# Head squares on ScalarE, a shared second query half, absorbed queries behind the prompt attention, and the gate third applied last

## What is computed

```
shift, scale, gate = split(silu(c) @ w_ada + b_ada)
h = rms(x) * (1 + scale) + shift
zq, zkv, zd, ga, gb, ma, mb = split(h @ w_in)
q      = rms(zq) @ w_qb            # 8 heads of 64 + 32, each part normalised, the 32 rotated
rows   = [rms(zkv[:256]), rope(rms(zkv[256:]))]        # latent and rotary key
dq, dk = rope(rms(zd)), dv = zd    # 3 dilated groups, 4 heads of 64
k_nope = rms(rows @ w_uk); v = rows @ w_uv
o_a    = attention(q, [k_nope, k_pe])   # prompt: causal; sample: 4096 cached rows per sequence
o_b    = dilated window attention over the 3 groups, combined
y      = x + gate * ((sigmoid(ma) * ((o_a*silu(ga)) @ w_pa) + sigmoid(mb) * ((o_b*silu(gb)) @ w_pb)) @ w_out)
```

## Time and profile before

| what | value |
|---|---|
| median of 3 runs | 1371.1 us (1368.76 to 1372.58) |
| time of the profiled execution | 1372.51 us |
| its span | 1370.7 us |
| mean granted TensorE clock | 0.913 |
| busy: PE, DVE, ACT, POOL | 89%, 52%, 36%, 19% of the span |
| chain that ended last, by engine | PE 57%, DVE 19%, issue 8%, ACT 5%, DMA 5%, POOL 4% |

### The profile page before, as it was taken

One profiled execution on the slowest core, in us unless ns is written; L12 is line 12 of the kernel. 1 busy time (PEld: TensorE's weight loads), 2 busy tenths in 40 slices (PEclk: granted clock), 3 DMA queues, 4 the chain that ended last, 5 costly groups with the idle time before them and its releaser, 6 DMA issues.

```text
span 1370.7 us, 22960 instructions
## 1 busy us (share of the span) xinstructions
PE 1219.1 (89%) x7616; PEld 998.1 (73%) x7616; DVE 715.8 (52%) x1657; ACT 495.2 (36%) x1159; POOL 254.7 (19%) x252
## 2 busy tenths in 40 slices
PE   5987758998897899999987999998999899997986
PEld 1277647786786678778765998988999899997431
DVE  4137887456865233030322676766676667676422
ACT  1133334332243333322322554545454545453010
POOL 0023330048865012333431000000000000000000
PEclk9989857999999657999998999999999999998579
DMA  8622010031242102233264310323232323225005
GB/s 262 220 77 72 23 41 1 13 81 47 73 127 77 31 23 71 77 101 85 71 199 159 96 31 22 88 62 88 61 86 64 88 61 83 66 75 184 1 20 166
DMA packets 79398, 112.24 MB, mean 82 GB/s; under 512 B 8627, under 2 KB 50756, under 8 KB 79293
## 3 DMA queue, kind: packets, MB, share of 16 engines
q1 hardware_dynamic: 76214, 101.59, 25.8%
q0 software_dynamic: 1440, 5.11, 1.0%
q10 hardware_dynamic: 1648, 4.23, 0.8%
HBM read 105.21 MB, written 5.68 MB: 81 GB/s over the span
## 4 chain that ended last, share of the span: by engine, by line
PE 57%; DVE 19%; issue 8%; ACT 5%; DMA 5%; POOL 4%; SPq 2%; ACTq 0%; DVEq 0%; POOLq 0%
PE ps L1376 18%; PE ps L1050 5%; PE ps L1051 5%; PE ps L1052 5%; PE ps L1357 5%; DVE ssq L2106 3%; PE ps L1065 3%; PE ps L1402 3%; DMA raw<-in_w_ada 2%; ACT cT_hi L850 2%; PE ps L1422 2%; PE ps L1212 1%; PE ps L1255 1%; POOL tmp L946 1%; PE ps L1266 1%
## 5 line engine op out<-in xcount | busy, mean ns | idle before, releaser
L931 POOL TENSOR_TENSOR wlo<-raw,whi 128x512 fp32r<-128x512 f32 (+3 forms) x148 | 172.1, 1165 | 459.8 <-ACT whi L620 459.6
L1376 PE MATMUL ps<-wq_hi,cT_hi 128*128 128x260 f32 x1024 | 217.8, 294 | 0.5 <-ACT sq L879 0.5
L1050 PE MATMUL ps<-whi,hT_hi 128*128 128x512 f32 (+3 forms) x512 | 190.3, 372 | 30.4 <-POOL wlo L931 19.2
L2106 DVE TENSOR_REDUCE ssq<-sq 128x8 f32<-128x512 f32 x256 | 172.6, 682 | 66.6 <-ACT sq L879 64.5
L1376 PE MATMUL ps<-wq_hi,cT_lo 128*128 128x260 f32 x1024 | 206.3, 283 | 0.0
L1376 PE MATMUL ps<-wq_lo,cT_hi 128*128 128x260 f32 x1024 | 206.0, 282 | 0.0
L620 ACT ACTIVATE whi<-raw 128x512 fp32r<-128x512 f32 (+3 forms) x148 | 83.3, 564 | 316.5 <-PE ps L1047 246.3
L1052 PE MATMUL ps<-whi,hT_lo 128*128 128x512 f32 (+3 forms) x512 | 185.8, 363 | 0.0
L1051 PE MATMUL ps<-wlo,hT_hi 128*128 128x512 f32 (+3 forms) x512 | 185.7, 363 | 0.0
L1376 PEld LDWEIGHTS ps<-wq_hi,cT_hi 128*128 128x128 f32 x1024 | 157.6, 190 | 1.1 <-ACT sq L879 1.1
L1376 PEld LDWEIGHTS ps<-wq_hi,cT_lo 128*128 128x128 f32 x1024 | 158.2, 189 | 0.0
(11 more groups left out here) (390 smaller groups left out, 1690.0 us busy)
## 6 DMA issues: line engine op xcount, KB each, us to landing
cn<-in_cache_mla SPq DMA_DIRECT2D x256, 144.0 KB, 2.1
raw<-in_w_in SPq DMA_DIRECT2D x64, 256.0 KB, 2.7
raw<-in_w_ada SPq DMA_DIRECT2D x48, 256.0 KB, 3.0
raw<-in_w_out SPq DMA_DIRECT2D x32, 256.0 KB, 3.0
sdk<-in_cw SPq DMA_DIRECT2D x3, 1536.0 KB, 11.0
raw<-in_w_in SPq DMA_DIRECT2D x32, 128.0 KB, 2.0
raw<-in_w_pa SPq DMA_DIRECT2D x16, 256.0 KB, 2.9
x_tiles<-in_x_prompt ACTq DMA_DIRECT2D x4, 512.0 KB, 5.6
```

Source lines behind the costliest of these rows:

```text
L931: nc.gpsimd.tensor_tensor(out=wlo[:, s % NHL, 0:width], in0=raw[:, j % NRAW, 0:width], in1=whi[:, s % NHL, 0:width].bitcast(F32), op=ALU.s ...
L1050: mm(out, hi[:, k, c], bh, start=st, stop=False)
L1376: last = mm(ps[:, 3 + 2 * (u % 2) + f, 0:260], a[c], wq[:, c, f, w], start=c == 0 and a is hi and wq is wq_hi, stop=c == 1 and a is lo)
L2106: v.tensor_reduce(out=ssq[:, (4 * g + u) * 8:(4 * g + u + 1) * 8], in_=sq4[:, u, :].rearrange("p (h e) -> p h e", e=NOPE), axis=AX, op=ALU ...
```

## The change

Four things are done:

- **Gate third last.** Shift and scale are turned once `ada0` to `ada3` are in; `ada4` and `ada5` follow on PE, and h is computed meanwhile. The gate matmuls and their two copies move behind the dilated projections. `gate_bc` now shares its memory with `wukT`, and `k_s` shares that of `dq_s`.
- **Squares on ScalarE.** For the prompt tiles of QB0, K, QB1 and the DgQK, ACT squares its own staged copy into one of two buffers, and DVE only sums. The sample tile stays on DVE. ACT also makes the rotary copies of the keys, and DVE rotates the key rows of the four prompt tiles at once.
- **Second query half shared.** POOL finishes tiles 1 and 3 of QB1 with `finish_q`, DVE tiles 0, 2 and TS, after it has scaled all five in the order 1, 0, 3, 2, TS.
- **Absorbed queries later.** The transposes stand behind the prompt attention, the 16 matmuls ahead of the fourth chunk of `D0QK`, and DVE's part behind the attention.

```diff
-          + [("gate", 2, "A"), ("Q", 5, "A"), ("KV", 5, "A"), ...
+          + [("Q", 5, "A"), ("KV", 5, "A"), ...
-STAGES += [("TD", 4 * (ND - 1), "A"), ...
+STAGES += [("gate", 2, "A"), ("TD", 4 * (ND - 1), "A"), ...
...
+            def to_stage_squared(idx, w):
+                k = staged[0]
+                to_stage(idx, w)
+                squared_[0] += 1
+                n = squared_[0]
+                act.wait_ge(evac_a, READER[idx][1])
+                if n > 2:
+                    act.wait_ge(square_free, n - 2)
+                nc.scalar.activation(squares[n % 2][:, 0:w], stage[:, k % NSTAGE, 0:w], ACT.Square).then_inc(squared, 1)
...
-            for n in range(2, 6):
+            for n in range(2, 4):
                 to_stage(ITEM[f"ada{n}"], 512, n=NB + 1)
-            split_to(FIRST["Q"] + NHL)
-            for n in range(2):
-                copy_out(ITEM["gate"] + n, gate_bc[:, n * 512:(n + 1) * 512], 512)
             for k in range(KD):
                 act.wait_ge(h_f, k + 1)
                 nc.scalar.activation(hThi[:, k, :], xT[:, k, :], ACT.Copy).then_inc(h_hi, 1)
+            for n in range(4, 6):
+                to_stage(ITEM[f"ada{n}"], 512, n=NB + 1)
...
+            act.wait_ge(rows_ready, 4)
+            for t in range(NT):
+                nc.scalar.activation(kc[:, t, :].rearrange("p (h e) -> p h e", e=QK)[:, :, NOPE:QK],
+                                     rep(rows[:, t, KVR:CW], 1, HM), ACT.Copy).then_inc(kc_rope, 1)
             for t in range(NT):
-                to_stage(ITEM["K"] + t, 512)
+                to_stage_squared(ITEM["K"] + t, 512)
...
                 for t in range(NT):
-                    to_stage(ITEM[f"D{g}QK"] + t, 512)
+                    to_stage_squared(ITEM[f"D{g}QK"] + t, 512)
...
+            finish_q(1, 1, Q_FREED + 10 + 1, qh1_pool, 1)
+            finish_q(1, 3, Q_FREED + 10 + 3, qh1_pool, 2)
...
+            def absorbed_queries(k):
+                if k != 3:
+                    return
+                misc_begin()
+                for odd in range(2):
+                    ...                       # the same 16 matmuls as before
             for g in range(ND):
-                block_of(f"D{g}QK", ITEM[f"D{g}QK"], range(5), hThi, hTlo, hTs)
+                block_of(f"D{g}QK", ITEM[f"D{g}QK"], range(5), hThi, hTlo, hTs,
+                         ahead_of=absorbed_queries if g == 0 else None)
...
+            for n in range(2):
+                idx = ITEM["gate"] + n
+                wait_bank(idx)
+                mm(ps[:, idx % BANKS, :], ident[0:NB + 1, NB:NB + 1].to_broadcast([NB + 1, P]),
+                   gate_s[:, n * 512:(n + 1) * 512], start=True, stop=True).then_inc(z_done, 1)
             heads_turned(0, ITEM["TD"])
...
-                link(v.tensor_tensor(out=sqt[0:n, :], in0=z, in1=z, op=ALU.mult))
-                link(v.tensor_reduce(out=ms[0:n, 8 * t:8 * t + 8], in_=sqt[0:n, :].rearrange("p (h e) -> p h e", e=64),
-                                     axis=AX, op=ALU.add))
+                sq3 = head_sums(t, z, 512).rearrange("p (h e) -> p h e", e=64)
+                sums_read(t, v.tensor_reduce(out=ms[0:n, 8 * t:8 * t + 8], in_=sq3, axis=AX, op=ALU.add))
...
-                for t in range(5):
+                for t in ((1, 0, 3, 2, TS) if i else range(5)):
                     q_item(i, t, zs[t])
+                if i:
+                    for n, t in enumerate((0, 2, TS)):
+                        q_finish(t, n + 1)
```

More of the change, by code:

```diff
@@ L753, in _ @@
             for t in range(NT):
[L754 removed]
+                squared_[0] += 1
+                n = squared_[0]
+                if n > 2:
+                    act.wait_ge(square_free, n - 2)
+                act.wait_ge(evac_a, READER[ITEM["QB0"] + t][1])
+                nc.scalar.activation(squares[n % 2][:, 0:384], stage[:, (k0 + t) % NSTAGE, 0:384], ACT.Square)\
+                  .then_inc(squared, 1)
+            act.wait_ge(rows_ready, 4)
+            for t in range(NT):
+                nc.scalar.activation(kc[:, t, :].rearrange("p (h e) -> p h e", e=QK)[:, :, NOPE:QK],
+                                     rep(rows[:, t, KVR:CW], 1, HM), ACT.Copy).then_inc(kc_rope, 1)
+            for t in range(NT):
+                to_stage_squared(ITEM["K"] + t, 512)
             to_stage_small(ITEM["K"] + TS, 512)
@@ L1671, in _ @@
             low_h(KD - 1)
+            for n in range(4, 6):
+                ada_item(n)
             v.tensor_tensor(out=g96[:, 0:NOPE], in0=gn[:, G_QN:G_QN + 64], in1=gn[:, G_KN:G_KN + 64], op=ALU.mult)
@@ L1847, in _, with set_q @@
             attention(MLA_JOBS, 0, 0, 4, 2, mla_mask, mla_place, MLA_SCALE)
+            misc_wait()
+            v.tensor_copy(qsT[:, :], ps[:, 7, 0:32])
+            link(v.memset(qpe[:, :], 0.0))
+            for u in range(4):
+                last = v.tensor_copy(qpe[32 * u:32 * u + 32, :].rearrange("p (b u h) -> p u h b", b=NB, u=4)[:, u],
+                                     ps[0:ROPE, 7, 32:96].rearrange("p (h b) -> p h b", b=NB))
+            misc_read(last)
+            misc_wait()
+            misc_read(v.tensor_copy(qabs[:, 0:NB * 16].rearrange("p (b c h) -> p c h b", c=2, b=NB),
+                                    ps[:, 7, 0:128].rearrange("p (c h b) -> p c h b", c=2, b=NB)))
+            link(v.memset(qabs[:, NB * 16:(NB + 1) * 16], 0.0))
+            def set_q(b, p, step):
+                q3 = qabs[:, bass.ds(16 * b, 16)].rearrange("p (c f h) -> p c f h", c=2, f=2)
+                cols_ = slice(260 * p, 260 * p + 4)
+                step(v.tensor_copy(wq_hi[:, :, :, cols_], q3))
+                return v.tensor_tensor(out=wq_lo[:, :, :, cols_], in0=q3, in1=wq_hi[:, :, :, cols_].bitcast(F32),
+                                       op=ALU.subtract)
+            for b in range(2):
+                link(set_q(b, b, link))
+            dve.wait_ge(kc_ready, 5)
+            own = tmp_t[0:NB, 1792:2560]
+            link(v.tensor_tensor(out=own, in0=q_s[:, :], in1=k_s[:, :], op=ALU.mult))
+            link(v.tensor_reduce(out=dns[:, :], in_=own.rearrange("p (h e) -> p h e", e=QK), axis=AX, op=ALU.add))
+            link(v.tensor_tensor(out=snew[:, :].rearrange("p (b h) -> p b h", b=NB), in0=rep(dns[:, :], 1, NB),
+                                 in1=rep(newmask, 2, HM), op=ALU.add))
             for g in range(ND):
```

176 lines of the change are left out of this document (92 added, 84 removed).

## The result

The changed kernel takes 1365.31 us (median of 18 runs, 1360.88 to 1370.61) against 1369.58 us for the kernel before (18 runs beside them, 1366.48 to 1374.36): a ratio of 0.9963, 95% interval 0.9952 to 0.9974. The forecast was 1346, with a range of 1337 to 1358. The profiled execution took 1366.24 us, its span is 1364.4, 6.3 us shorter than that of the kernel before, where -24.8 was forecast.

What follows compares the result with a forecast made beforehand. The chain named PE over most of the span, but PE was not the bound in three places the edit touches. Terms -6.4 -13.5 -12.9 +5 +0 +3 = -24.8 took 1372.5 to 1347.7, median 1346 us, range 1337 to 1358.

Steps and rivals of the forecast that it cites:

- Part 2: Key rows and squares moved to ScalarE, up to the second query half's rsqrt: terms summing to -13.5 us.
- Part 3: Last rsqrt to first attention mask: finishing shared with GpSimd and absorbed queries moved out, -12.9 us (-8 to -15).
- Part 4: Absorbed queries moved behind attention and into the first dilated block, where PE is the bound: +5 us (+4.1 to +8.5).
- Part 5: Dilated squares on ScalarE: 0 for each of the first two groups (-0.7 to +2.7 us).
- Part 6: Third dilated group with the gate matmuls behind it: +3 us (+1 to +5).
- the same, shifted: After 430 us the trace was expected unchanged apart from its shift in time; no term in the sum.
- Part 1: Gate third behind h: first projection matmul at 75.4 against 81.81 us, -6.4 us (-4.6 to -7.9).
- so both last blocks end 1.3 us later: Last two modulation blocks: delayed 1.3 us by the transposes and weight stream, bounds 0 and 3.1.
- Rival A: Second query half's tail: VectorE and GpSimd fully take turns, 13.7 instead of 10.6 us; +5, total 1351; chance 0.15.
- a share for a clock that falls: First dilated block: allowance within the +5 us for PE's clock falling behind the thin absorbed-query work.
- Rival B: ScalarE paces the dilated groups: three rotations each 2.7 us later, absorbed matmuls 7.2; +8 +3, total 1357; chance 0.13.
- Rival D: Prompt attention stays at half clock, starting straight out of idle: up to 36 us more, 1382; chance 0.04.

Runs made afterwards that it cites:

- e5: Changed kernel with the squares of the three dilated groups back on VectorE; median 1357.70 us, ratio 0.9912 to the kernel before.
- e9: Changed kernel with the sixteen shift and scale transposes moved inside the fifth modulation block, ahead of its third chunk; 1363.89 us, ratio 0.9947.
- e7: Changed kernel without GpSimd's finishing of the first query half (work left out), single run; key rsqrt to the next one 12.2 us against 16.4.
- e2: Changed kernel with GpSimd's three weight-low splits held until VectorE has finished its tiles of the second query half; 1362.99 us, ratio 0.9952.
- e6: Changed kernel with all five tiles of the second query half finished by VectorE, none by GpSimd; 1361.75 us, ratio 0.9934.
- e12: The kernel of e10 with GpSimd's two shared tiles given back to VectorE; 1346.08 us, ratio 0.9823.
- e4: Changed kernel with the 16 absorbed-query matmuls moved to the sixth and seventh chunks of the second dilated block; 1358.28 us, ratio 0.9917.
- e3: Changed kernel with the two gate matmuls and their copies moved to just ahead of the first output-projection block; 1366.47 us, ratio 0.9974.
- e10: Changed kernel with the edits of e2, e4, e5 and e9 together; 1346.10 us, ratio 0.9812.
- e11: Kernel before with 82 tiny memsets (50 and 32) ahead in VectorE's program, single run; loop turns 131.2 and 131.2 us, before 130.3 and 130.1.
- e1: Changed kernel with 46 tiny memsets ahead of VectorE's first operation; 1361.07 us, ratio 0.9930.
- e8: Changed kernel with 90 tiny memsets (55 ahead of VectorE's first operation, 35 behind), single run; loop turns 130.6 and 131.3 us.

## Why the prediction was wrong

Four steps of it failed by 3.6 us or more, each below in its part: the stalls that GpSimd's work costs VectorE (parts 2 and 3), the absorbed matmuls in a block that PE bounds together with its clock (part 4), the squares on ScalarE put at 0 in the dilated groups (part 5, and by e5 most of part 6), and "the same, shifted" for the sample loop.

**Part 1, right in sign, 1.8 us short.** The step "so both last blocks end 1.3 us later" failed: it was 3.1, my upper bound (3.6 counted from the fourth addition), because the buffers stood full during a wait of 1.5 us for the addition as well as 1.4 us of turning. e9 shows that this is nearly all of it: its trace gets 3.3 back. The slow start of the first projection matmuls, which I had kept, stayed.

**Part 2, -9.9 for -13.5.** The squares and copies did leave VectorE: first query half -2.3 as predicted, second -3.4 against 3.1. The rows and the transposes behind them gave -2.1 for -3.1. The rest was missing at the keys (-1.2 for -3.1 with the rsqrt, -1.1 for -1.9 in the items): their sums gave -1.5 for -2.1, the rsqrt +0.3 for -1. I had written that the rsqrt would lose some of its stalls; it had 5.6 us where e7, without GpSimd beside it, has 2.9.

**Part 3, -8.9 for -12.9.** The sum took GpSimd's two tiles as 3 us saved with 2 us of stalls, and named two splits ahead of them but no splits behind. There were three, and each held up VectorE for about 1 us (e2: 2.8). The two tiles themselves were worth less than nothing: given back, the mask came 0.5 us earlier in e6 and 0.7 in e12. From the first item to its last finish VectorE alone had needed 11.0 us for five tiles (187.96 to 198.95); with the share it needed 13.6 (173.51 to 187.11), against a forecast of 8.1 and 2 of stalls. Rival A had 13.7, with a chance of 0.15; that it came so near is in part luck, since it priced full turn-taking over the two tiles and 2.8 us of the 13.6 are the splits behind them. The whole gain of this part is the absorbed queries that left the tail.

The Trainium skill, "SBUF — State Buffer", section Who interferes with whom, says that a VectorE instruction with two SBUF inputs, or a copy or scalar operation in its two-port mode, contends with GpSimd for a shared pair of ports that only one of them holds at a time (the two-input form with a GpSimd instruction that reads SBUF), while a reduction does not. The traces agree: 1.37, 1.51, 1.25 for two-input instructions and, in e6, 1.14, 1.19 for two with one input (0.18 alone), each beside a GpSimd subtraction of 1.3, while the reductions of the second query half took the same 0.42 us beside GpSimd's rotations as in e7 without them. I had quoted half of that rule and priced it as a rival instead of as a term.

**Part 4, +8.8 for +5.** The +5 held 0.7 for small transposes, which stand a row higher in the table (+0.9), so 4.3 was meant for the block. The 16 absorbed-query steps took 5.1 us (two groups of 16 matmuls, 1.95 each at full clock), and the half-clock stretches before and behind them the rest: these are the windows of the changed kernel in that block:

```profile
235.50:240.50 5.00, 3.86 (x40) 3.71 (x40) 1.54 (x7) 1.14 (x3) 0.00 (x0) 1.00 0.00 0
240.50:245.50 5.00, 5.00 (x20) 3.93 (x17) 1.51 (x6) 0.00 (x0) 0.00 (x0) 0.66 0.02 3
...
250.50:255.50 5.00, 4.94 (x32) 4.27 (x32) 0.00 (x0) 0.63 (x1) 1.73 (x2) 0.91 0.15 36
255.50:260.50 5.00, 5.00 (x16) 4.30 (x17) 2.92 (x8) 0.00 (x0) 0.00 (x0) 0.50 0.06 18
260.50:265.50 5.00, 5.00 (x21) 4.03 (x21) 0.34 (x2) 0.63 (x1) 1.29 (x1) 0.91 0.00 0
```

PE came to the block at full clock, fell to 0.66 in its first 5 us, and was at 0.50 behind the absorbed matmuls. The term "a share for a clock that falls", 0.5 in the sum, failed. The matmuls with the clock behind them cost 5.6 us in e2 and e9, near the 4.3; another 3.1 is half clock that came and went between executions of the same work. e4 shows that the 5.6 was avoidable, since PE's waits a block later took the matmuls in; that its block also started at full clock can't be put down to its edit.

**Part 5, +3.7 for 0.** Rival B's mechanism was right and its price of 8 too high. The first rotation of a group starts 17.9 us after the first evacuation (293.88 after 276.01) instead of 16.8 (353.48 after 336.64). The step that failed let VectorE pay that back; it did so for half of it in the first group (+0.6) and not at all later (+1.1 and +2.1, the last from e5).

**Part 6, +0.8 for +3.** The stretch grew by 2.9, which meets the forecast by luck: by e3 and e5 the gate is 0.8 of it and the squares 2.1.

**After 430 us I expected "the same, shifted".** That sentence cost 4.2 us, the loss of the loop, which no term covered. Between 423 and 834 the changed kernel gained 0.9 us that no edit explains: the stretch from the GA table load to the next one is 18.1 us in some executions (before, e4, e10, e12) and 17.0 to 17.7 in the others (17.2 in the changed kernel, 17.1 in e11, which is the kernel before with pads).

**Rival D** put up to 36 us on an attention that stays at half clock. PE is busy 39.7 of the 42 us from 221 on in the kernel before, so its bound was some 4 us low; it did not come. The attention had its clock at 0.89 and took 51.5 us with the transposes, against 50.6.

The 18.5 us between forecast and span are, down the table, 1.8 + 3.6 + 4.0 + 0.9 + 3.8 + 1.7 - 0.1 - 0.9 + 4.2, and -0.5 behind the loop. What the runs took off one by one was 3.3 (e9), 4.2 (e7, by leaving out work), 2.8 (e2), 8.7 (e4, of which 5.6 is shown to be its edit), 3.7 (e5) and 4.5 (e1), all counted in the stretches and not in the medians. Why the place of the loop costs time stays open, and so do the difference of 0.9 us at GA and the clock at the start of the first dilated block.

## What to carry to other kernels

The time of work given to GpSimd beside a busy VectorE is not simply taken off VectorE: here each collision with a subtraction made one VectorE instruction about 1 us longer, the finishing of five tiles (16 us on GpSimd) cost VectorE 4.2 us, and two shared tiles gained nothing. Look also at what stands behind the shared work in GpSimd's queue. Small matmuls belong where PE already waits for data; in a block that PE bounds 3.9 us of them cost 5.6 here, with the clock that fell behind them. Before a change of the clock is put down to an edit, look for it in the traces of other kernels that run the same work up to there. When an edit changes how many instructions stand ahead of a hardware loop, follow one group through the loop in both traces and compare the instruction queues, and try a pad of memsets before explaining a difference by the edit.

## What was not expected of the hardware

- The place of a loop in VectorE's program changes the time of a turn by 2.2 us (132.3 against 130.1 us), with nothing shown but an unexplained gap and more packets on one instruction queue (51 against 41). Kernels with the same number of VectorE instructions ahead of the loop as the changed one (e2, e3, e4, e7, e9) all show 50 packets and turns of 132.2 to 133.6 us. The packets alone don't set the time: e8 has 51 and turns in 130.6 and 131.3.
- Five tiles finished by VectorE alone take 7.7 us, three beside a busy GpSimd 7.9.
- The granted clock in the first 5 us of the same block was 0.66 in some executions (changed, e1, e3, e5, e6, e8) and 1.00 in others (e2, e9) with the same PE work; the block took 35.5 or 32.3 us accordingly.
